# Expert weights of a hybrid decoder step: two pairs of buffers and a single one made into a ring of five sets, with the expert loops written out

## The reference

```python
def hier_moe(h, lw):
    ...
    comb = jnp.sum(jax.nn.one_hot(eid, MOE_EXPERTS, dtype=jnp.float32) * wts[..., None], axis=1).astype(h.dtype)
    out = jnp.zeros_like(h)
    for e in range(MOE_EXPERTS):
        act = jax.nn.silu(h @ lw['w_exp_gate'][e]) * (h @ lw['w_exp_up'][e])
        out = out + comb[:, e:e + 1] * (act @ lw['w_exp_down'][e])
    return out
```

## Time and profile before

| | before |
|---|---|
| median of 3 runs | 885.23 us (885.2 to 887.98) |
| the profiled execution | 886.53 us |
| its span | 884.7 us |
| PE busy | 794.8 us, 90% |
| PEld busy | 639.5 us, 72% |
| DVE busy | 505.2 us, 57% |
| ACT busy | 314.0 us, 35% |
| moved from and to HBM | 216.72 MB read, 15.37 MB written |

### The profile page before, as it was taken

The page is one execution under the profiler, slowest core; times in us unless marked ns, Lnnn a source line. Parts: engine busy times, 40 slices in busy tenths (PEclk is TensorE's granted clock), DMA queues, the critical chain, the costliest instruction groups (busy, mean ns, idle before and its releaser), DMA issues.

```text
span 884.7 us, 14773 instructions
## 1 busy us (share of the span) xinstructions
PE 794.8 (90%) x6020; PEld 639.5 (72%) x6020; DVE 505.2 (57%) x915; ACT 314.0 (35%) x618; POOL 37.3 (4%) x50
## 2 busy tenths in 40 slices
PE   4899999999899998899998899999979977877865
PEld 4899999899777786578865799998945534443422
DVE  4463889584789539797868557576441323212312
ACT  4444545354343343544663745343321101000100
POOL 0000000000101001012111000000000000000000
PEclk9999999999999999899999999999959999888977
DMA  9335455365526347798899595856848899999965
GB/s 374 120 112 229 154 182 189 116 246 185 191 96 226 131 169 269 239 315 284 291 351 390 159 358 193 312 185 229 324 209 337 331 422 423 422 422 422 420 254 206
DMA packets 36397, 231.92 MB, mean 262 GB/s; under 512 B 3920, under 2 KB 4200, under 8 KB 12384
## 3 DMA queue, kind: packets, MB, share of 16 engines
q1 hardware_dynamic: 28512, 199.56, 58.1%
q0 software_dynamic: 7824, 31.51, 11.0%
HBM read 216.72 MB, written 15.37 MB: 262 GB/s over the span
## 4 chain that ended last, share of the span: by engine, by line
PE 61%; DVE 15%; DMA 14%; SPq 4%; ACT 3%; issue 2%; POOL 0%; DVEq 0%; ACTq 0%; POOLq 0%
PE bank L553 15%; PE bank L925 13%; PE bank L541 8%; DMA M<-in_w_exp_up 6%; PE bank L1065 4%; SPq L1209 4%; DMA M<-in_w_exp_down 3%; PE bank L1079 3%; PE bank L592 3%; PE bank L562 2%; DVE at_r L235 2%; PE bank L1026 2%; DMA W<-in_w_in 1%; DVE M L1903 1%; PE bank L625 1%
## 5 line engine op out<-in xcount | busy, mean ns | idle before, releaser
L235 DVE TENSOR_TENSOR at_r<-W,at_r 128x1024 fp32r<-128x1024 f32 x100 | 121.2, 1222 | 96.8 <-ACT at_r L1406 64.1
L541 PE MATMUL bank<-HN,W 128*128 128x264 f32 x640 | 156.2, 399 | 2.6 <-DMA W<-in_w_in 2.6
L541 PEld LDWEIGHTS bank<-HN,W 128*128 128x128 f32 x640 | 124.0, 196 | 28.8 <-issue 3.6
L553 PE MATMUL bank<-at_r,at_r 128*128 128x264 f32 (+1 forms) x1152 | 141.5, 284 | 2.2 <-DVE M L1742 2.2
L553 PEld LDWEIGHTS bank<-at_r,at_r 128*128 128x128 f32 x1152 | 140.1, 188 | 3.0 <-DVE at_r L235 2.4
L925 PE MATMUL bank<-at_r,at_r 128*128 128x264 f32 x960 | 120.7, 287 | 5.2 <-DVE at_r L235 5.2
L925 PEld LDWEIGHTS bank<-at_r,at_r 128*128 128x128 f32 x960 | 119.1, 191 | 5.9 <-DVE at_r L235 5.8
L1382 ACT ACTIVATE M<-bank 128x264 f32<-128x264 f32 (+4 forms) x110 | 43.2, 407 | 165.0 <-PE bank L541 85.6
L1065 PE MATMUL bank<-M,W 128*32 128x256 f32 x1024 | 71.1, 442 | 31.4 <-DMA M<-in_w_exp_up 28.6
L1065 PEld LDWEIGHTS bank<-M,W 128*32 128x32 f32 x1024 | 36.3, 127 | 65.2 <-DMA M<-in_w_exp_up 31.1
L1406 ACT ACTIVATE at_r<-W 128x1024 fp32r<-128x1024 f32 x60 | 62.4, 1053 | 17.3 <-PE bank L553 13.2
(11 more groups left out here) (355 smaller groups left out, 987.7 us busy)
## 6 DMA issues: line engine op xcount, KB each, us to landing
W<-in_w_in SPq DMA_DIRECT2D x42, 1024.0 KB, 5.0
M<-in_w_exp_gate SPq DMA_DIRECT2D x32, 1024.0 KB, 21.1
M<-in_w_exp_up SPq DMA_DIRECT2D x32, 1024.0 KB, 26.0
M<-in_w_exp_down SPq DMA_DIRECT2D x28, 1024.0 KB, 18.0
W<-in_w_mem_kv SPq DMA_DIRECT2D x8, 1024.0 KB, 7.1
M<-in_mem_kT SPq DMA_DIRECT2D x8, 1024.0 KB, 6.2
M<-in_state_ssm POOLq DMA_DIRECT2D x8, 1024.0 KB, 9.1
out_s_ssm<-M POOLq DMA_DIRECT2D x8, 1024.0 KB, 7.2
```

The source lines that it names most:

```text
L235: return eng.tensor_tensor(low, x, high.bitcast(F32), ALU.subtract)
L541: mm = pe.matmul(bank[:, 0:n], w[:, k, P * c:P * (c + 1)], x[:, k, 0:n], start=(k == 0), stop=(k == KT - 1))
L553: mm = pe.matmul(bank[:, 0:n], w[:, k, :], x_[:, k, 0:n], start=(k + i == 0), stop=(k == KT - 1 and i == 2))
```

## The change

Four things are done.

1. **Ring.** On the path of one round the loads take the sets in turn. The order of the loads stays; load n goes into the set whose use is number n-5 in the order of use (g0, u0, g1, u1, d0, g2, u2, d1, g3, ...). So g2 waits for g0 and u2 for u0 as before, but d1 waits for g1, g3 for u1, u3 for d0, d2 for g2, and so on; d7 waits for u6 (and d5). The other path keeps the old places.
2. **Written out.** `steps` writes all 8 quads out on every engine, with constants in place of registers, and SP's loads are written out too.
3. **Halves apart.** `gathered_stored` becomes one semaphore for each half. The 4 transposes of half 0 wait for its copy alone, those of half 1 for theirs; the gate matmuls of k 0 to 3 wait for the copy of half 0 and those of k 4 to 7 for that of half 1.
4. **Norm factors moved.** The six small matmuls leave `gather` and stand in `gate_up` between gate and up; ACT copies `RSLOT` right before its SiLU. One semaphore `norm_up_filled` counts these and the up matmuls; DVE's `find_slots` for the next quad waits for it too.

The second half of d7 counts on the semaphores of gate and up (two pieces each), and its matmuls (`last_down`) wait for them in two pairs. `down_in` becomes two semaphores. The semaphore `route_args` is folded into `chosen`.

```diff
+        ring_sets = [free1, free2, free3, free4, free5]
+        ring_loads = [("gate", 0), ("up", 0), ("down", 0), ("gate", 1), ("up", 1)]
+        ring_uses = [("gate", 0), ("up", 0)]
+        for q in range(2, QUADS + 1):
+            if q < QUADS:
+                ring_loads += [("gate", q), ("up", q)]
+            ring_loads.append(("down", q - 1))
+            ring_uses += [("gate", q - 1), ("up", q - 1), ("down", q - 2)]
+        ring_home = {load: ring_sets[n] for n, load in enumerate(ring_loads[:5])}
+        for used, load in zip(ring_uses, ring_loads[5:]):
+            ring_home[load] = ring_home[used]
...
             if rounds == 1:
-                step(0, 0)
-                with eng.Fori(0, QUADS // 2 - 1) as it:
-                    step(1, it * 2 + 1)
-                    step(0, it * 2 + 2)
-                step(1, QUADS - 1)
+                for q in range(QUADS):
+                    step(q % 2, q)
...
-                if silus is None:
-                    pe.wait_ge(drained[0], uses[0])
-                else:
-                    pe.wait_ge(sem("silu"), silus)
-                for t, rows in enumerate((P, P, BATCH_S)):
-                    pe.matmul(psum[0][:, 256:258], ONE[0:rows, t].rearrange("p j s -> p (j s)"),
-                              RTOK[0:rows, t:t + 2], start=(t == 0), stop=(t == 2))
-                pe.wait_ge(sem("gathered_stored"), 5 * n + 2)
-                for k in range(KT):
-                    mm = pe.transpose(psum[4 + k // 4][:, P * (k % 4):P * (k % 4 + 1)], DOWNED[:, P * k:P * (k + 1)], ident)
-                    if k % 4 == 3:
-                        mm.then_inc(sem(f"gathered{k // 4}"), 1)
+                for half, per_quad in enumerate((2, 2)):
+                    pe.wait_ge(sem(f"gathered_stored{half}"), per_quad * n + 1)
+                    for k in range(4):
+                        mm = pe.transpose(psum[4 + half][:, P * k:P * (k + 1)],
+                                          DOWNED[:, 512 * half + P * k:512 * half + P * (k + 1)], ident)
+                    mm.then_inc(sem(f"gathered{half}"), 1)
...
                 def gate_up(buf, q, n):
-                    pe.wait_ge(sem("gathered_stored"), 5 * (n + moved) + 5)
...
                         for k in range(KT):
+                            if kind == "gate" and k % 4 == 0:
+                                pe.wait_ge(sem(f"gathered_stored{k // 4}"), 2 * (n + moved) + 2)
...
-                        mm.then_inc(sem(f"{kind}_filled"), 1)
+                        mm.then_inc(sem("gate_filled" if kind == "gate" else "norm_up_filled"), 1)
+                        if kind == "gate":
+                            for t, rows in enumerate((P, P, BATCH_S)):
+                                mm = pe.matmul(psum[0][:, 256:258], ONE[0:rows, t].rearrange("p j s -> p (j s)"),
+                                               RTOK[0:rows, t:t + 2], start=(t == 0), stop=(t == 2))
+                            mm.then_inc(sem("norm_up_filled"), 1)
...
+                if rounds == 1:
+                    for used, (kind, q) in zip(ring_uses, ring_loads[5:-1]):
+                        set_used(*used)
+                        for j in range(QUAD):
+                            load_piece(kind, q * QUAD + j, q, j, piece(kind, q, j, True))
+                    set_used(*ring_uses[len(ring_loads) - 6])
+                    set_used("down", QUADS - 3)
...
                 def gate_silu(n, which):
-                    act.wait_ge(sem("gate_filled"), n + 1)
+                    act.wait_ge(sem("norm_up_filled"), 2 * n + 1)
+                    a.activation(RSLOT[which], psum[0][:, 256:257], ACT.Copy).then_inc(sem("silu"), 1)
+                    act.wait_ge(sem("silu"), 2 * n + 1)
                     a.activation(SG, psum[0][:, 0:D_FF], ACT.Silu, scale=RSLOT[which]).then_inc(sem("silu"), 1)
...
                     if not is_last(q):
                         dve.wait_ge(sem("slots_ready"), q + 1)
+                        dve.wait_ge(sem("norm_up_filled"), 2 * q + 1)
                         find_slots(q + 1, q + 1)
```

More of the change, by code:

```diff
@@ L302, in build_program, with piece @@
         assert y_end + 6 * PIECE <= MAP["Z"][0]
-        def piece(kind, q, j):
-            o = {"gate": (free1, free4)[q % 2], "up": (free2, free5)[q % 2], "down": free3}[kind][j]
+        ring_sets = [free1, free2, free3, free4, free5]
[9 more added lines that the diff above has]
+            ring_home[load] = ring_home[used]
+        def piece(kind, q, j, ring=False):
+            o = (ring_home[kind, q] if ring else
+                 {"gate": (free1, free4)[q % 2], "up": (free2, free5)[q % 2], "down": free3}[kind])[j]
             return M[:, o:o + PIECE].rearrange("p (k n) -> p k n", n=512 if kind == "down" else D_FF)
@@ L443, in build_program @@
         up_in = [sem(f"up_in{b}") for b in range(2)]
-        down_in = sem("down_in")
+        down_in = [sem(f"down_in{b}") for b in range(2)]
+        landed_all = 16 * QUAD * (QUADS // 2)
         def by_rounds(eng, experts):
@@ L1016, in _, with gather @@
             full(pe.matmul(b[:, 0:32], ones_r[0:8, :], m2, start=False, stop=True), "total")
-            def gather(n, silus=None):
+            def gather(n):
                 pe.wait_ge(sem("slots_found"), n + 1)
@@ L1074, in turn, with down @@
                     mm.then_inc(sem("act_turned"), 1)
-                def down(half, buf, which):
+                def down(half, buf, q, which):
                     for f in range(FF_T):
@@ L1080, in down, with last_down @@
                                            ACTT[which][:, f, SLOTS * j:SLOTS * (j + 1)],
-                                           piece("down", buf, j)[:, FF_T * half + f, :], start=(f == 0), stop=(f == 1))
+                                           held("down", buf, q, j)[:, FF_T * half + f, :], start=(f == 0), stop=(f == 1))
                     mm.then_inc(sem(f"down_filled{half}"), 1)
+                def last_down(buf, q, which):
+                    for arrived, count, pieces in ((gate_in[0], 32, (0, 1)), (up_in[0], 32, (2, 3))):
+                        pe.wait_ge(arrived, landed_all + count)
+                        for f in range(FF_T):
+                            for j in pieces:
+                                mm = pe.matmul(psum[3][SLOTS * j:SLOTS * (j + 1), :],
+                                               ACTT[which][:, f, SLOTS * j:SLOTS * (j + 1)],
+                                               held("down", buf, q, j)[:, FF_T + f, :], start=(f == 0), stop=(f == 1))
+                    mm.then_inc(sem("down_filled1"), 1)
                 def back(half, n):
@@ L1098, in finish @@
                     mm.then_inc(sem("back_filled"), 1)
-                    pe.wait_ge(down_in, q * (16 * QUAD) + 16 * QUAD)
+                    pe.wait_ge(down_in[buf], (q - buf) * (16 * QUAD // 2) + 16 * QUAD)
                     pe.wait_ge(sem("actT_ready"), n + 1)
-                    down(0, buf, which)
+                    down(0, buf, q, which)
                     if is_last(q):
@@ L1104, in finish @@
                         back(0, n)
-                        pe.wait_ge(sem("last_half_in"), 16 * QUAD)
-                        down(1, buf, which)
+                        last_down(buf, q, which)
                     else:
-                        down(1, buf, which)
+                        down(1, buf, q, which)
                         pe.wait_ge(sem("back_ready"), n + 1)
@@ L1115, in step @@
                     if not is_last(q):
-                        gather(q + 1, q + 1)
+                        gather(q + 1)
                     turn(q)
@@ L1129, in experts @@
                 if rounds > 1:
-                    pe.wait_ge(sem("gathered_stored"), 5)
+                    for half in range(2):
+                        pe.wait_ge(sem(f"gathered_stored{half}"), 2)
+                pe.wait_ge(drained[0], uses[0])
                 steps(pe, rounds, step, alone)
@@ L1206, in _, with load_piece @@
                 r += 1
-            def load_piece(kind, e, q, j):
+            def load_piece(kind, e, q, j, dst=None):
                 src = ins[f"w_exp_{kind}"][e].rearrange("p (k f) -> p k f", f=512 if kind == "down" else D_FF)
-                sp.dma_start(piece(kind, q, j), src).then_inc(
-                    {"gate": gate_in[q % 2], "up": up_in[q % 2], "down": down_in}[kind], 16)
+                sp.dma_start(piece(kind, q, j) if dst is None else dst, src).then_inc(
+                    {"gate": gate_in[q % 2], "up": up_in[q % 2], "down": down_in[q % 2]}[kind], 16)
             for n in range(number[("swa", 0)], len(chunks)):
@@ L1264, in next_pieces, with set_used @@
                     else:
-                        sp.wait_ge(sem(f"{kind}_filled"), (q - 1) * rounds)
+                        name, per_quad = {"gate": ("gate_filled", 1), "up": ("norm_up_filled", 2)}[kind]
+                        sp.wait_ge(sem(name), (q - 1) * (rounds * per_quad))
                     for j in range(QUAD):
```

(18 more changed lines are left out.)

29 lines of the change are left out of this document (15 added, 14 removed).

## The result

| | before | changed |
|---|---|---|
| median | 885.22 us (884.95 to 887.98, 4 runs) | 873.18 us (872.86 to 873.31, 4 runs) |
| the profiled execution, its span | 886.53, 884.7 us | 872.86, 870.7 us |
| ratio, 95% interval | | 0.9857, 0.9837 to 0.9876 |

The change makes the kernel 12.0 us faster; 873.1 was forecast. Later comparisons, on four chips, have the kernel before between 882.8 and 890.2 us from run to run.

A forecast was written before the change was run, and what follows sets the result against it. The stream of weights, at 421 GB/s, was taken to bound the experts. Terms of 2.24, 4.83, 2.35 and 2.73 us sum to 12.15 us, giving 873.1 us from a median of 885.23; range 871.0 to 878.0.

The forecast's parts named there:

- What bounds: In the experts the stream of weights, at 421 GB/s, sets the pace; the PE has 32.7 us to spare.
- Start of g2: Gate matmuls of quad 0, and g2's issue behind them, come 2.24 us earlier; lower end 1.3 us.
- The hole behind u2: Pause of the stream between u2 and d1, closed since d1 waits for g1's matmuls: 4.83 us.
- The hole in front of d7: Pause between d6 and d7: only the PE's wait of 2.35 us returns, 6 us of the closed hole unused.
- Clock in the last quad: Without the wait for d7, the PE's clock stays at 1.00 in the last quad: 2.73 us, or 0.
- Writing out: Straight code for all 8 quads in place of loops gains and costs nothing: 0 us.
- The sum: All terms of the change together: 12.15 us off the median of 885.23 us, giving 873.1 us.

The follow-up runs named there:

- e5: The changed kernel with d1 held until the down matmuls of quad 0 are done; ratio 0.9933 to the kernel before, median 882.88 us.
- e1: The kernel before with the quads and SP's loads written out, nothing else; ratio 1.0012 to the kernel before, median 888.01 us.
- once more: The changed kernel run again without any edit; ratio 0.9855 to the kernel before, median 874.13 us.
- e4: The changed kernel with d7 held until the down matmuls of quad 6 are done; ratio 0.9912 to the kernel before, median 879.02 us.
- e3: The changed kernel without the ring, its loads with their old places and waits; ratio 0.999 to the kernel before, median 887.19 us.
- e6: The changed kernel with d6 loaded ahead of u7, PE and DVE order to match; ratios 0.9779 and, repeated, 0.9804 to the kernel before.
- e2: The kernel before, written out and with the ring, gather and norm factors in the old order; ratio 0.9901 to the kernel before, median 878.25 us.
- e7: The changed kernel with 20 unread matmuls in the PE's wait for the routing; ratio 0.9814 to the kernel before, median 870.52 us.

## Why the prediction was right, and where it was not

- *What bounds.* Right: 420 GB/s from 683 to 843, and the gap that e5 brought back was paid in full, while e1's code changed nothing that can be told.
- *Start of g2*: 2.24 forecast, ends 1.3 and 2.24. **The term was mis-sized.** The gate starts 7.32 us behind the gather where it took 9.63, 2.3 less, as worked out. But gather to g2 fell by 4.72, because the 64 gate matmuls ran wholly at full clock. I had taken it that the gate matmuls raise the clock and the work ahead does not; in the changed kernel the clock rose during the transposes ahead of them (columns as in rows 2):

```profile
655.40:657.30 1.90, 1.78 (x9) 1.41 (x9) 0.77 (x2) 0.60 (x1) 0.00 (x0) 0.62 0.00 0
657.30:661.00 3.70, 3.69 (x65) 2.46 (x65) 0.61 (x1) 0.00 (x0) 0.00 (x0) 1.00 0.01 2
```

That early rise does not follow from the edit alone: of the seven profiles with this order and no filled wait three had the gate in 3.66 us (changed, once more, e4), and e3, e5 and both of e6 in 5.41 to 5.63. With these gates, partly at the low clock, the term is 2.7 to 3.0, so the upper end I gave was too low in either case.
- *The hole behind u2*: 4.83 forecast, 4.11 in g2 to d6 against before, 4.94 of e2 against e1, 6.3 of e5 against the changed kernel. Right mechanism; the size goes with how fast g2 and u2 came in ahead of it, see below.
- *The hole in front of d7*: 2.35 forecast, 2.78 measured, of which 0.35 are d6's matmuls in 4.99 for 5.34 us. The rest, 2.4, is the wait (2.36 in the earlier trace rows). That most of the 9 us would stay unused was right, and e6 shows the reason was: with finish 6 moved ahead of the last full set, 4 us and more came out.
- *Clock in the last quad*: 2.73 forecast, 2.50 measured, from d7 to the last group. The 0.20 behind it are not the clock's: the last 8 `back` take 2.39 us in both, and the far branch there 3.91 us for 4.18. e4 returned wait and low clock together. The four profiles with a wait in front of d7 (before, e1, e3, e4) need 9.41 to 11.58 us from d7 to the last group, and the five others of the table 7.73 to 7.76.
- *Writing out*: 0 forecast, 0.12% in e1 with an interval that holds zero. The DMA queue that brings instructions moved 50 packets in e1 and 49 in the changed kernel, for 43 before.
- *The sum.* 12.15 forecast, 12.04 between the medians. Between the profiled executions it is 13.7: the start came out 2.5 larger, the hole behind u2 0.7 smaller, and before's execution was 1.3 slow. The span is 870.7 where 872.6 was forecast. The largest error, the start, rests on where the clock happened to rise, so that the median was met to 0.1 us is luck; that it fell within a few us is not.

## What to carry over

Where a stream of transfers sets the pace, list its pauses and ask for each what is late once it is closed: a pause in the middle is worth its length, one near the end only what the engine behind it really waited for. A free buffer is the one used up next, not the one of the same kind. When the last arrivals leave an engine with a tail of work, order the last loads so that the one with the shortest work behind it comes last.

## What the runs showed of the hardware

- **An idle wait is not all that moves the clock.** In front of d6 the PE waits 1.9 to 3.4 us in every profile of the table; behind it 32 down matmuls took 4.95 to 6.59 us in seven of nine and 3.64, full clock, in e2 (wait 2.40) and e7 (wait 2.49). And in e7 the clock fell at 647.3, with the PE idle for no more than 0.8 us at a time ahead of it (busy 2.50 of the 3.70 us from 644.3 to 648.0), and stayed low under a PE that was busy 5.80 of 5.80 us. The Trainium skill, TensorE: Matmul & The Clock Gate, "Part 1: The HAM clock gate (the "warmup" mystery)", says that the same kernel meets it differently from run to run. These traces agree: the up matmuls of quad 7 took 6.54 us in one profile of the changed kernel and 5.15 in the other.
- **The first set came in slower on the old order.** From 2 to 10 us behind g2's issue, the core took 373, 383 and 376 GB/s in before, e1 and e2, and 416 to 426 in the ten other profiles, all with the small matmuls moved. In before and e1 that makes the gap behind u2 shorter than e5's: from 20 to 30 us behind g2's issue the mean is 220 GB/s in before, 213 in e1 and 164 in e5. What causes it was not tried and stays open.
- **Straight code under a full stream shows no cost here.** Over eight written-out quads, with 421 GB/s passing, e1's time lies within -0.07 and +0.32% of the looped kernel's.
